# Modulation sums of groups 2 to 10 moved from VectorE to ScalarE and GpSimd

## The reference, cut to what matters

```
mod = silu(c) @ ada_w[l] + ada_b[l]              # 2048 -> 3 * 2048, two layers
shift, scale, gate = split(mod, 3)
h = rms_norm(x, norm_g[l]) * (1 + scale) + shift
... products of h with w_in, attention, convolution, w_pw, w_out ...
x = x + gate * y

mod = silu(c_2) @ w_ada_2[0] + b_ada_2[0]        # 2048 -> 6 * 2048, third layer
```

## Time and profile before

| | |
|---|---|
| time, median of 3 runs | 2408.45 us (2408.14 to 2411.93) |
| span of the profiled execution | 2405.4 us from its first to its last instruction |
| busy: TensorE matmuls | 2242.7 us, 93% |
| busy: VectorE | 1791.1 us, 74% |
| busy: ScalarE | 924.6 us, 38% |
| busy: GpSimd | 52.6 us, 2% |
| pieces of groups 2 to 10 on VectorE (line 994) | 288, 364.2 us |
| `w_lo` on VectorE (line 1026) | 564, 675.6 us |
| mean rate of all transfers | 232 GB/s |

### The profile page before, as it was taken

How to read it: one execution, slowest core, us unless ns; L and a number is a source line. 1 busy time by engine, 2 the same in 40 slices (tenths; PEclk the granted TensorE clock), 3 DMA queues, 4 the chain that set the end, 5 groups by cost and what they waited for, 6 DMA issues and landing times.

```text
span 2405.4 us, 41562 instructions
## 1 busy us (share of the span) xinstructions
PE 2242.7 (93%) x16273; PEld 2137.8 (89%) x16273; DVE 1791.1 (74%) x2404; ACT 924.6 (38%) x1355; POOL 52.6 (2%) x63
## 2 busy tenths in 40 slices
PE   3299999998989998999999999899999999999998
PEld 2298997788989977899999997689999999999998
DVE  6897998797979987978867867768885656644444
ACT  2154404224634042354443432255543444434343
POOL 0000000000000000023000000000000000000000
PEclk7599999999999999999999999899999999999998
DMA  9988955696988466959948984257875555555553
GB/s 336 361 277 284 304 150 201 226 326 199 309 282 283 137 232 216 333 156 273 370 145 300 360 299 151 95 168 251 275 257 166 183 183 183 183 158 182 180 185 108
DMA packets 413233, 557.39 MB, mean 232 GB/s; under 512 B 25139, under 2 KB 362103, under 8 KB 412868
## 3 DMA queue, kind: packets, MB, share of 16 engines
q1 hardware_dynamic: 409536, 550.70, 69.3%
q0 software_dynamic: 1120, 2.18, 0.5%
q10 hardware_dynamic: 2468, 3.07, 0.4%
HBM read 553.72 MB, written 2.17 MB: 231 GB/s over the span
## 4 chain that ended last, share of the span: by engine, by line
PE 77%; DVE 10%; DMA 7%; issue 4%; ACT 2%; SPq 0%; DVEq 0%; ACTq 0%
PE gemm L1473 70%; DMA w_raw<-in_w_in 4%; DVE ada_acc L994 2%; DMA ada_first<-in_ada_w 2%; PE stat L1493 2%; DVE w_lo L1026 1%; ACT w_hi L708 1%; PE bankO L1544 1%; DVE ss L1221 1%; DMA ada_raw<-in_w_ada 1%; DVE ada_acc L1013 0%; PE bankS L1647 0%; PE bankS L1646 0%; DVE q_tok L1228 0%; DVE k_tok L1228 0%
## 5 line engine op out<-in xcount | busy, mean ns | idle before, releaser
L1026 DVE TENSOR_TENSOR w_lo<-w_raw,w_hi 128x1024 fp32r<-128x1024 f32 (+1 forms) x564 | 675.6, 1210 | 391.2 <-ACT w_hi L708 388.1
L1473 PE MATMUL gemm<-h_hi,w_hi 128*128 128x256 f32 (+2 forms) x3056 | 871.3, 285 | 19.2 <-DVE h_lo L1071 13.9
L1473 PE MATMUL gemm<-h_hi,w_lo 128*128 128x256 f32 (+2 forms) x3056 | 868.5, 284 | 0.0
L1473 PE MATMUL gemm<-h_lo,w_hi 128*128 128x256 f32 (+2 forms) x3056 | 868.4, 284 | 0.0
L708 ACT ACTIVATE w_hi<-w_raw 128x1024 fp32r<-128x1024 f32 (+1 forms) x564 | 571.8, 1028 | 650.1 <-PE gemm L1473 540.1
L1473 PEld LDWEIGHTS gemm<-h_hi,w_hi 128*128 128x128 f32 (+2 forms) x3056 | 587.4, 192 | 21.0 <-issue 16.5
L1473 PEld LDWEIGHTS gemm<-h_lo,w_hi 128*128 128x128 f32 (+2 forms) x3056 | 587.5, 192 | 0.5
L1473 PEld LDWEIGHTS gemm<-h_hi,w_lo 128*128 128x128 f32 (+2 forms) x3056 | 587.2, 192 | 0.3
L994 DVE SCALAR_TENSOR_TENSOR ada_acc<-ada_raw,c_act,ada_acc 128x1024 f32<-128x1024 f32 x288 | 364.2, 1278 | 5.6 <-DMA ada_raw<-in_w_ada 3.0
L1473 PE MATMUL gemm<-G_hi,w_hi 128*128 128x256 f32 x704 | 200.7, 285 | 3.1 <-DVE w_lo L1026 3.1
L1473 PE MATMUL gemm<-G_hi,w_lo 128*128 128x256 f32 x704 | 200.4, 285 | 0.0
(11 more groups left out here) (294 smaller groups left out, 2703.8 us busy)
## 6 DMA issues: line engine op xcount, KB each, us to landing
w_raw<-in_w_in SPq DMA_DIRECT2D x264, 512.0 KB, 5.7
w_raw<-in_w_up SPq DMA_DIRECT2D x176, 512.0 KB, 3.6
ada_raw<-in_ada_w SPq DMA_DIRECT2D x160, 512.0 KB, 6.9
ada_raw<-in_w_ada SPq DMA_DIRECT2D x160, 512.0 KB, 5.1
w_raw<-in_w_out SPq DMA_DIRECT2D x96, 512.0 KB, 6.3
w_raw<-in_w_down SPq DMA_DIRECT2D x64, 512.0 KB, 3.7
ada_first<-in_ada_w SPq DMA_DIRECT2D x32, 512.0 KB, 8.8
ada_late<-in_w_ada SPq DMA_DIRECT2D x32, 512.0 KB, 4.3
```

What stands on the lines that cost most here:

```text
L1026: dve.tensor_tensor(w_lo[:, fixed % PARTS, 0:sz], w_raw[:, fixed % RAW, 0:sz], w_hi[:, fixed % PARTS, 0:sz].bitcast(F32), ALU.subtract).th ...
L1473: last = pe.matmul(half(g, k, q), left, right, start=(kt == 0 and j == 0), stop=(u == len(g.units) - 1 and t == nk - 1 and j == len(parts) ...
```

## The change

Groups 0, 1 and 11 stay on VectorE. For groups 2 to 10, each of the 288 pieces is now done in two steps: ScalarE multiplies the piece in place by its per-partition number (a `Copy` activation with `scale` taken from `c_act`), and GpSimd adds it to the accumulator. GpSimd also clears all accumulators from group 2 on. The products `ua`, `ub`, `kb`, `vb`, `ka`, `va` and `oa` are written out in full (four blocks in the body) instead of as a loop with two blocks in the body, because GpSimd's code for a group is written out in full and does not loop with them. The slots, their number, the loads and their order are unchanged.

```
-ZEROED_EARLY = (2,)
-ZEROED_POOL = (5, 11)
+DVE_GROUPS = (0, 1, 11)
...
-            G["ua", l] = product("ua", wi, 4, CB, full, 2, "a", h_hi, h_lo,
-                                 lambda i, k, B: O_U + i * CB + (1 - k) * DC, ada=(2 + 3 * l, 16, 1))
+            G["ua", l] = product("ua", wi, 4, CB, full, 4, "a", h_hi, h_lo,
+                                 lambda i, k, B: O_U + k // 2 * CB + (1 - k % 2) * DC, ada=(2 + 3 * l, 16, 1))
...
+            def ada_zero(n, free):
+
+                pool.wait_ge(*free)
+                pool.memset(acc_of(n)[:], 0.0).then_inc(pool_zeroed, 1)
+                pool.wait_ge(pool_zeroed, n - 1)
+
+            def ada_sum(n, j0=0, j1=AU):
+
+                for j in range(j0, j1):
+                    pool.wait_ge(ada_scaled, AU * (n - 2) + j + 1)
+                    if j >= 2:
+                        pool.wait_ge(ada_used, AU * n + j - 1)
+                    acc = acc_of(n)[:, j % 2 * AC:(j % 2 + 1) * AC]
+                    pool.tensor_tensor(acc, acc, ada_raw[:, j % ASLOTS, :], ALU.add).then_inc(ada_used, 1)
+                pool.wait_ge(ada_used, AU * n + j1)
...
             pool.wait_ge(mask_done, 1)
+            ada_zero(2, summed_by(0))
             for l in range(LAYERS):
+                ada_sum(3 * l + 2)
+                ada_zero(3 * l + 3, summed_by(3 * l + 2))
+                ada_sum(3 * l + 3)
                 wait_out(pool, G["pw", l])
                 link(pool.memset(qrT[ROPE:P], 0.0))
                 pool.memset(krT[ROPE:P], 0.0).then_inc(rope_padded, 1)
                 pool.wait_ge(rope_padded, l + 1)
+                ada_zero(3 * l + 4, summed_by(3 * l + 3))
+                ada_sum(3 * l + 4)
                 if l + 1 < LAYERS:
-                    pool.wait_ge(gap_summed, l + 1)
-                    pool.memset(ada_acc[:], 0.0).then_inc(ada_zeroed, 1)
+                    ada_zero(3 * l + 5, (gap_summed, l + 1))
...
+            pool.wait_ge(bias_masked, 2)
+            ada_zero(8, (gap_summed, 2))
+            ada_sum(8)
+            ada_zero(9, (o_read, NH * 3))
+            ada_sum(9)
+            ada_zero(10, summed_by(8))
+            ada_sum(10, 0, AU // 2)
+
             wait_out(pool, G["mg"])
...
-            pool.wait_ge(gap_summed, 3)
-            pool.memset(ada_acc[:], 0.0).then_inc(ada_zeroed, 1)
+            ada_sum(10, AU // 2)
+            ada_zero(11, (gap_summed, 3))
...
+            def ada_scale(n, j, m, fixed, rounds):
+
+                slot = fixed % ASLOTS
+                act.wait_ge(ada_loaded[slot], rounds * 16)
+                act.activation(ada_raw[:, slot, :], ada_raw[:, slot, :], ACT.Copy,
+                               scale=c_act[:, 0 if n < 6 else 1, m:m + 1]).then_inc(ada_scaled, 1)
...
@@ prep of ScalarE
                         act.activation(w_hi[:, fixed % PARTS, 0:sz], w_raw[:, fixed % RAW, 0:sz],
                                        ACT.Copy).then_inc(w_hi_done, 1)
+                    for piece in ada_pieces(before, u, len(g.units)):
+                        if piece[0] not in DVE_GROUPS:
+                            ada_scale(*piece)
                     if beside is not None:
...
@@ prep of VectorE
                     for piece in ada_pieces(before, u, len(g.units)):
-                        ada_add(*piece)
+                        if piece[0] in DVE_GROUPS:
+                            ada_add(*piece)
...
@@ through, VectorE
-                if g.ada is not None and g.ada[1] == 0:
-                    if g.ada[0] in ZEROED_POOL:
-                        dve.wait_ge(ada_zeroed, g.ada[0] + 1)
-                    elif g.ada[0] not in ZEROED_EARLY:
-                        ada_zero(g.ada[0])
+                if g.ada is not None and g.ada[0] in DVE_GROUPS:
+                    dve.wait_ge(pool_zeroed, g.ada[0] - 1)
```

More of the change, by code:

```diff
@@ L237, in program @@
         ada_zeroed = sem("ada_zeroed")
+        ada_scaled = sem("ada_scaled")
+        pool_zeroed = sem("pool_zeroed")
         const_loaded = sem("const_loaded")
@@ L352, in program @@
         G["qb"] = product("qb", w2, 4, CB, full, 2, "a", h_hi, h_lo, plain(O_QB))
[L353 to L354 removed]
+        G["kb"] = product("kb", w2, 4, CB, full, 4, "a", h_hi, h_lo, plain(O_QB + DC), ada=(8, 0, 1))
+        G["vb"] = product("vb", w2, 4, CB, full, 4, "b", h_hi, h_lo, plain(O_QB + 2 * DC), ada=(8, 16, 1))
         G["qa"] = product("qa", w2, 4, CB, full, 4, "a", h_hi, h_lo, plain(0))
[L356 to L358 removed]
+        G["ka"] = product("ka", w2, 4, CB, full, 4, "a", h_hi, h_lo, plain(O_KA), ada=(9, 0, 1))
+        G["va"] = product("va", w2, 4, CB, full, 4, "b", h_hi, h_lo, plain(O_VA), ada=(9, 16, 1))
+        G["oa"] = product("oa", w2, 4, CB, full, 4, "a", h_hi, h_lo, plain(O_OA), ada=(10, 0, 1))
         G["mg"] = product("mg", w2, 1, 4 * NHA, full, 1, "s", h_hi, h_lo, plain(O_G))
@@ L816, in gate_of_u @@
                 def gate_of_u(i, k, g, l=l, p0=p0):
-                    if k == 1:
+                    if k % 2:
                         return
                     wait_full(act, g, i, k)
-                    wait_read(act, g, i - 1, 1, 1)
+                    if k:
+                        wait_read(act, g, i, k - 1, 1)
+                    else:
+                        wait_out(act, G["krope", l] if g is G["ua", l] else G["ua", l])
                     for q in range(2):
-                        ins = act.activation(sig[:, q, :], half(g, k, q), ACT.Sigmoid,
-                                             bias=par[:, bass.ds(i * 2 + p0 + 78 + q + (4 if g is G["ub", l] else 0), 1)])
-                        freed(ins, g, k)
+                        c = p0 + 78 + q + k + (4 if g is G["ub", l] else 0)
+                        freed(act.activation(sig[:, q, :], half(g, k, q), ACT.Sigmoid, bias=par[:, c:c + 1]), g, k)
                 ahead(act, G["ua", l], prep, lambda i, k: gate_of_u(i, k, G["ua", l]))
@@ L1153, in _ @@
             mod_out(0)
-            ada_zero(2)
             mod_out(1)
@@ L1166, in value_of_u @@
                     first = 4 if g is G["ub", l] else 0
-                    if k == 0:
+                    if k % 2 == 0:
                         return
                     wait_full(dve, g, i, k)
-                    wait_read(dve, g, i, 0, 1)
+                    wait_read(dve, g, i, k - 1, 1)
                     for q in range(2):
-                        dst = u_pad[:, bass.ds(i * 2 + q + first, 1), TAPS - 1:UW].rearrange("p a b -> p (a b)")
-                        ins = dve.scalar_tensor_tensor(out=dst, in0=half(g, k, q),
-                                                       scalar=par[:, bass.ds(i * 2 + p0 + 70 + q + first, 1)],
+                        c = k - 1 + q + first
+                        ins = dve.scalar_tensor_tensor(out=u_pad[:, c, TAPS - 1:UW], in0=half(g, k, q),
+                                                       scalar=par[:, p0 + 70 + c:p0 + 71 + c],
                                                        in1=sig[:, q, :], op0=ALU.add, op1=ALU.mult)
```

16 lines of the change are left out of this document (9 added, 7 removed).

## The result

The changed kernel takes 2538.29 us (2534.61 to 2539.43, 4 runs) against 2409.67 us (2408.14 to 2411.93, 4 runs) of the kernel before: a ratio of 1.053, 95% interval 1.0515 to 1.0545, some 129 us slower. The forecast was 2474 us. The sign is as predicted, and the mechanism as far as it goes; the loss is twice as large, above the forecast's own range (2430 to 2520 us) and inside the wide one (2400 to 2560).

The account below looks back on a forecast made before the run. VectorE and transfers were taken as near their limit in `lat` to `ua`, VectorE's pieces as costly in `q` and `pw`, TensorE as bound in `kb` to `oa`. Terms 40+10+6+4+7−2 = +65 on 2405.4, plus 3.05: 2474 us; range 2400 to 2560.

Parts of the forecast that it names:

- The exclusion: Wherever pieces are added: GpSimd's adds and VectorE's `w_lo` take turns, each waiting for the whole of the other.
- an add of 2.7 us: Upper bound for GpSimd's add, two reads and a write one after another: some 90 us more, 2564 us.
- the slots rival: In `outca` and `outcb`, ScalarE's waits for pieces make a unit 6.8 us: +32 a layer, 2532 us; chance 0.16.
- The price of a pair: One GpSimd add of 2.18 us plus 0.94 for `w_lo`: 3.12 us, against 2.33 for VectorE alone.
- I had taken 20: `lat` to `ua`, twice: +20 us each, between +15.6 with no turn lost and +24 with VectorE's idle time added.
- the terms of +4 and +7: `kb` and `vb`: last piece late, +4 us (0 to +8); `ka` to `oa`: first gate row late, +7 (0 to +15).
- `q` and `pw`: +5: `q` and `pw`, twice: turns of 56 us against 49.7 now, +5 us each, from −5 to +12.
- `outca` and `outcb`: +3: `outca` and `outcb`, twice: slots hold back units where attention is over, less relief of VectorE; +3 us, −5 to +16.
- the five microseconds of relief: `outca` and `outcb`: 4.9 us of pieces leave a stretch of 10.4 in which VectorE sets the pace.
- `out2b`: −2: `out2b`: 6.2 us of pieces leave the chain, ScalarE's step of 1.15 us joins it; −2 us, −6 to +6.
- The cheap add: Rival: the add costs 1.16 us or takes no turn, deciding at 1.39; −27 us, 2381 us; chance 0.14.
- Cancelling: Rival: relief in `q`, `pw` and `outcb` balances an add of 1.6 us or so; 2408 us, chance 0.05.

Follow-up runs that it names:

- no add: The changed kernel with each GpSimd add replaced by a memset of one column, sums of groups 2 to 10 left out: 2394.78 us.
- write only: The changed kernel with each GpSimd add replaced by three chained memsets, as long as an add but reading nothing: 2424.94 us.
- no scaling: The changed kernel without ScalarE's scaling, GpSimd adding the pieces as they were loaded: 2526.62 us.

## Why the prediction was right in kind and half in size

**The exclusion: right, and shown.** Both its signs came (`w_lo` 3.42 us beside adds, adds 3.39), and the run with memsets of the same length leaves `w_lo` at 1.225 us and takes 113 of the 129 us away. So it is in the main not GpSimd being slow, nor a semaphore, nor a slot. The Trainium skill ("SBUF — State Buffer", section "Who interferes with whom") excepts a GpSimd instruction that only writes from its rule for two on-chip inputs; the run agrees (1.225 us). The rule itself shows at the stages' ends as well (`m_lo` 3.3 to 3.4 us beside adds against 1.14).

The whole balance, from differences of runs: nothing from loops and clearing, −15 us from relief of VectorE with ScalarE's step included (no add), +30 from GpSimd's length (write only less no add), +113 from the turns. With the adds in place ScalarE's step is worth 12 of them at most by the medians (no scaling). The terms share effects, and each is good to some 5 to 8 us; the sign and order of size are what the runs carry.

**The time: missed, and where it hit, partly by luck.** 2538 us lies inside 2400 to 2560 because I had put the upper end there for an add of 2.7 us and for the slots. It lies 6 us from the slots rival's 2532, and neither condition came: the add takes 2.35 us, and `outca` and `outcb` lose 13 and 12 us where that rival had 32 each. Of the 67 us by which the table's sum exceeds mine, `ub` has 14, `outca` and `outcb` 19, `out2b` 14, `kb` to `vb` 9, `ka` to `mg` 7, and the other stages 4.

**The price of a pair: mis-sized.** I took 2.18 + 0.94 = 3.12 us; measured are 2.35 + 1.00 = 3.35. The estimate of the add from one-operand rows was 0.17 us low. The other 0.06 us are what a `w_lo` adds. In `lat` to `ua` that is 28 × 0.23 = 6 us, on top of the 15.6 of the full pairs alone: 22. I had taken 20, about half of VectorE's idle time being added instead, and met 20.8 and 22.2. Two errors of opposite sign made this term good.

**`kb` to `vb` and `ka` to `oa`: the terms of +4 and +7, measured +13.0 and +14.4.** The pair's price is the term that was off: 32 × 0.23 = 7.4 us and 44 × 0.23 = 10 us on my own sums give 11 and 17. So the method was right for these stages and its input was not. Where a stage's loss is the small difference of two long sums (99.8 against 95.6 us), 7% in a unit price nearly triples it. (The term of +7 was counted to the first gate row, which starts 14.4 + 1.1 = 15.5 us later.)

**`ub`: no term at all, measured +6.8 and +6.7** (at TensorE's 21st unit behind its sum). The sum has nothing for the 16 pieces of group 3 that run beside `ub`, although even my own pair of 3.12 us is longer than TensorE's 2.87. The chain of the changed kernel behind TensorE's sum at 238.42:

```profile
238.42 5.46 PE stat L1535 x32
...
248.50 3.36 DVE rstd L1223
...
251.89 6.79 DVE lat L1225 x6
258.68 15.54 DVE w_lo L1071 x6
```

TensorE starts on `ub` at once, at 247.5, with the units that were split ahead. Meanwhile VectorE works through the norm and six scalings before the next `w_lo`. The scalings take 6.79 us instead of 2.46, because the next group's adds already run beside them (GpSimd's first at 253.03). The first new `w_lo` starts at 258.60, 11.1 us behind TensorE's start, where it was 9.1 (236.28 − 227.20). It takes 1.21 us; those behind it take 3.42 us each, one every 3.35 us, and TensorE, at 2.87 us a unit, uses up its lead and then waits for them. A pair of 3.35 us is never hidden behind a unit of 2.87; the lead only puts the loss off.

**`q` and `pw`: +5, measured +6.0 and +5.3 (12.8 and 12.0 less the part of `ub`).** Right in size. The scalings that I had named as partners of the adds, from 436 to 493 us, compare:

```profile
L1270 DVE SCALAR_TENSOR_TENSOR q_tok<-q_tok,ss,g_qk 128x192 f32<-128x192 f32 x16 | 21.7, 1430 | 0.0
...
L1270 DVE SCALAR_TENSOR_TENSOR k_tok<-k_tok,ss,g_qk 128x192 f32<-128x192 f32 x16 | 9.3, 650 | 0.0
```

Each query scaling takes 1430 ns and each key scaling 650, where both took 410 before.

**`outca` and `outcb`: +3, measured +13.1 and +12.0.** I looked for the loss in the slots (5.8 us a unit) and priced the adds' turns at nothing, "few steps with two on-chip inputs". The slots are the smaller part: with memsets in place of adds the stages lose 3.6 and 5.8 us. The rest needs adds that read, and with the last eight pieces back on VectorE about half of the loss is gone (9.2 and 10.0 to 4.8 and 3.4): turns of the few steps that TensorE waits for at the end. The chain of the changed kernel there:

```profile
574.75 1.60 DVE w_lo L1071
576.35 3.27 DVE m_lo L1151
579.62 3.35 DVE w_lo L1071
582.97 3.33 DVE m_lo L1151
...
586.43 5.58 PE gemm L1515 x32
```

Four steps on the chain take 11.6 us; each such step takes 1.14 to 1.22 alone. And the five microseconds of relief that I had set against it do not show: the run without adds has −0.4 and −0.2.

**`out2b`: −2, measured +11.7.** The sign was wrong. I priced the relief and ScalarE's step but no turns, though the stage has its pieces beside the gate rows. From the chain of the changed kernel:

```profile
1546.51 2.35 POOL ada_acc L610
...
1550.50 5.28 DMA g_bias<-in_b_gates
...
1555.85 0.46 ACT i_row L957
...
1562.87 3.39 DVE b_row L1361 x2
...
1566.29 2.65 DVE i_row L1364
...
1568.97 3.31 DVE m_row L1366 x2
```

The gate row starts 10.1 us behind TensorE's sum at 1545.74 instead of 9.0 (1434.62 − 1425.58), since a piece stands ahead of the selector and the bias on GpSimd: 1.1 us. These three rows, five instructions on 4 partitions, take 9.35 us instead of 3.2 (1.27, 0.68 and 1.27 in the trace before, where no piece stood beside them on another engine): 6.1 us. The other 4.5 us of the stage I have not divided further. ScalarE's step is not the reason (11.9 us without it). Group 10 behind these rows alone came out at −2.1 us, the size that I had given the whole group, but that is within what two traces differ by.

**The rivals.** The cheap add is refuted: 2.35 us against the 1.39 at which it would decide. The slots as the bound are there, but small: 30 us of GpSimd's length in all stages. The sign that I had named for them did not come: SyncE waits 61.7 us for `ada_used` in `outca` and `outcb` (490 to 562 us), where it waited 59.1 before (456 to 530 us), and TensorE does not wait for ScalarE's scaling there. Cancelling is refuted.

**What I did wrong in one sentence:** I took the exclusion as a price of the dense stages, by throughput, priced its pair 0.23 us too low and forgot `ub`, and left it out wherever VectorE's load was light; but there single steps stand on TensorE's path, and each pays a turn of up to 2.35 us.

## What to carry to other kernels

Before work goes to GpSimd beside a busy VectorE, look for the few places where the two already overlap in the trace and price both together: if they exclude each other, the pair costs the sum, and, where VectorE is the bound, the move is a loss unless GpSimd's step alone (2.35 us here) is shorter than what VectorE saves (1.28). Then go down the chain of the light stages too: each short VectorE step there on which another engine waits pays up to one whole turn, so that what is given to GpSimd belongs behind those steps (here the last twelve pieces of group 10, which at least cost nothing), not beside them. A piece that passes through two in-order engines ties their lists together, which cost 36 us here even without GpSimd.

## What the runs showed of the hardware beside this

Not only steps with two operands grew. VectorE's groups in the changed kernel, 502 to 563 us, attention beside adds that follow one another closely:

```profile
L1137 DVE TENSOR_SCALAR logit<-logit,rsums 128x256 f32<-128x256 f32 x16 | 16.3, 1058 | 0.3
...
L1128 DVE TENSOR_REDUCE negmax<-logit 128x2 f32<-128x512 f32 x8 | 5.5, 686 | 0.3
L1129 DVE TENSOR_SCALAR negmax<-negmax 128x2 f32<-128x2 f32 x8 | 5.4, 676 | 0.3
L1167 DVE SCALAR_TENSOR_TENSOR xT<-gemm,mod,xT 128x256 f32<-128x256 f32 x12 | 5.2, 473 | 0.0
```

and the same groups in the kernel before, the first two over all attention, the others from 489 to 540 us:

```profile
L1094 DVE TENSOR_SCALAR logit<-logit,rsums 128x256 f32<-128x256 f32 x48 | 14.8, 350 | 0.9
L1086 DVE TENSOR_SCALAR negmax<-negmax 128x2 f32<-128x2 f32 x24 | 4.1, 169 | 0.8
...
L1124 DVE SCALAR_TENSOR_TENSOR xT<-gemm,mod,xT 128x256 f32<-128x256 f32 x10 | 4.3, 474 | 0.5 <-PE gemm L1473 0.5
L1085 DVE TENSOR_REDUCE negmax<-logit 128x2 f32<-128x512 f32 x4 | 2.7, 686 | 0.1
```

- A scaling by one number per partition grew from 350 to 1058 ns, and one of only two numbers per partition from 169 to 676 ns. Both means rose by 0.5 to 0.7 us, so that a step need not be long to be held up; single ones of these scalings took 0.35 us between adds and 2.52 with an add under way (from 529.24 us).
- A reduction over 512 numbers (686 ns before and after) and a step that takes one of its two inputs from TensorE's accumulator memory (474 ns before, 473 after) did not grow beside the same adds.
- GpSimd's memsets, 0.95 us for 1024 numbers, did not hold back `w_lo` at all (1.225 us), where its adds did at every turn.
- Halving GpSimd's instructions raised their sum beside VectorE from 2.97 to 3.18 us a piece: finer turns are no remedy where GpSimd's list, with the turns in it, sets the pace.
